# Output rows and probabilities turned by transposing transfers; the four score units of a tile in one block

## The chip, the cores and the metric

One core of a Trainium2 chip runs the whole program. The time is device microseconds from one launch to its end, a median over runs. Engines: TensorE (PE: products, and PEld, its weight loads), VectorE (DVE), ScalarE (ACT), GpSimd (POOL), and SyncE (SP), which here only issues transfers.

## The reference

One step of a one-layer decoder, for 2048 prompt tokens (16 tiles of 128) and 8 sample tokens:

```
u = rmsnorm(x) * g;  proj = u @ w_in          # 1024 -> 2832
GLA heads (4): per-token recurrence S = diag(a) S + k v^T, o = q S, in chunks; rmsnorm(o); * silu(gate)
window heads (8, two key heads): softmax over 128 keys back and a learned sink logit; * silu(gate)
h = x + concat(both) @ w_out;  y = rmsnorm(h) * g_final
```

It also returns the final states, keys and values. Tile n's window heads need the keys of tiles n-1 and n; the GLA state passes from tile to tile.

## The kernel before, in words

Each f32 operand of a large product is kept as two half-precision parts, hi and lo, and a product is three matmuls (`split_product`, L575 to L577: hi hi, hi lo, lo hi). All weights stay on chip. `iterations` runs `body(Tile(n))` for n = 0 to 14 on every engine, each engine in its own written order; semaphores tie them together (`Events`, `Ring`). Tile 0 has its own order (`early`), and the last tile is interleaved with the sample tokens after the loop.

In body t, PE projects the tile t+1 (`proj` of gqk, sq, sklow, gv, gg, sg) and does the attention of tile t between the projections, then the output projection of tile t (`out_proj`, two groups). The PSUM banks stand in three rings of two: `pj` for projections, `at_ring` for scores and outputs, `tr` for turned blocks. A block of a ring may be filled only when the block two places before it in the ring's list was read (`wait_free`), and the reader is named in the list: DVE for bc, sq and sklow, ACT for gqk, gv, gg and sg. `bc` (L580) spreads the inverse norms of tile t+2 over the partitions; `scale_u` and `split_u` make that tile's hi and lo input.

The window heads of a tile are four units of two heads. `scores` (L664) fills two units. DVE's `row_max` (L1587) moves the older keys in, scales and takes the maximum; ACT's `probs` (L1167) takes exponentials; PE turns the unit by a product with the identity (`turn_probs`, L686); ACT rounds the turned block to the hi part (`probs_hi`, L1176) and DVE takes the lo part and masks a copy (`take_pt`, L1608); `values` (L695) multiplies. There are two slots for units (u % 2), so units 0 and 1 pass before 2 and 3. The gated output rows are scaled by DVE (`scale_rows`, L1656), turned by PE (`turn_out`, L807), and split by ACT and DVE (`take_out`) into `ogT_hi` and `ogT_lo` for `out_proj`. SP loads x twice a tile (as rows for the norm, and transposed on the host), x again for the residual, and stores y.

## Time and profile before

| | before |
|---|---|
| median of 3 runs | 903.19 us (903.15 to 903.64) |
| the profiled execution | 904.62 us, span 902.8 us, mean granted clock 0.975 |
| PE busy | 881.7 us (98%) |
| PEld busy | 616.0 us (68%) |
| DVE busy | 687.9 us (76%) |
| ACT busy | 383.0 us (42%) |
| POOL busy | 77.5 us (9%) |
| chain that ended last | PE 88%, DVE 5%, issue 4%, DMA 2% |
| bytes moved | 56.55 MB, mean 63 GB/s |

Busy is the time in which an engine had an instruction of its own in flight; matmuls overlap, so a group's mean is longer than the step from one to the next. The chain that ended last is followed back from the last instruction through whatever released each step. Lines are those of the kernel printed above.

### The profile page before, as it was taken

The numbers are of one execution on the slowest core, as the hardware profiler recorded it, in microseconds if no ns is written. First come the engines' busy times: TensorE is split into PE (matmuls) and PEld (weight loads), VectorE is DVE, ScalarE is ACT, GpSimd is POOL, SyncE is SP. The second block draws the span as 40 slices with busy tenths as digits, with TensorE's granted clock in tenths as the row PEclk, the third lists the DMA queues.
The fourth block names the chain that finished last, engine by engine and source line by source line (L and its number), as shares of the span: only waits on it lengthen the run. The fifth ranks groups of instructions, "written<-read, shape, count | busy, mean of one in ns | idle before, by whom it ended". The sixth has DMA issues, their size and how long they took to land.

```text
span 902.8 us, 22427 instructions
## 1 busy us (share of the span) xinstructions
PE 881.7 (98%) x9066; PEld 616.0 (68%) x9066; DVE 687.9 (76%) x2223; ACT 383.0 (42%) x1008; POOL 77.5 (9%) x117
## 2 busy tenths in 40 slices
PE   7898999999999999999999999999999999999997
PEld 5884576675858576675858576675858676775775
DVE  5899678868787778868787777868777777876854
ACT  4564543435353443435353433534353533434411
POOL 0041010101010010101010000101010100101200
PEclk7999999999999999999999999999999999999976
DMA  9921002020110202020100202020200102020014
GB/s 376 379 95 71 1 2 94 2 94 1 47 50 1 94 1 95 2 95 1 64 32 6 89 2 95 2 94 1 92 5 25 71 2 94 2 74 25 3 71 155
DMA packets 15687, 56.55 MB, mean 63 GB/s; under 512 B 3746, under 2 KB 5210, under 8 KB 14561
## 3 DMA queue, kind: packets, MB, share of 16 engines
q1 hardware_dynamic: 15296, 55.05, 16.1%
q8 instruction: 72, 1.18, 0.5%
q14 instruction: 31, 0.25, 0.1%
q10 hardware_dynamic: 288, 0.07, 0.0%
HBM read 44.33 MB, written 10.78 MB: 61 GB/s over the span
## 4 chain that ended last, share of the span: by engine, by line
PE 88%; DVE 5%; issue 4%; DMA 2%; ACT 1%; POOL 0%; SPq 0%; POOLq 0%; DVEq 0%
PE bank L575 24%; PE bank L577 23%; PE bank L576 23%; PE bank L766 3%; PE bank L680 3%; PE bank L692 2%; PE bank L815 1%; PE bank L788 1%; PE bank L792 1%; PE bank L629 1%; PE bank L752 1%; DVE w_in_hi_lo L1758 1%; PE bank L803 1%; DMA w_out_hi<-in_w 1%; DMA x_rows<-in_xq 1%
## 5 line engine op out<-in xcount | busy, mean ns | idle before, releaser
L575 PE MATMUL bank<-u_hi,w_in_hi_lo 128*128 128x128 f16 (+1 forms) x1288 | 208.5, 214 | 3.6 <-DVE w_in_hi_lo L1758 2.8
L577 PE MATMUL bank<-u_hi,w_in_hi_lo 128*128 128x128 f16 (+1 forms) x1288 | 208.1, 214 | 0.0
L576 PE MATMUL bank<-u_lo,w_in_hi_lo 128*128 128x128 f16 (+1 forms) x1288 | 208.1, 214 | 0.0
L575 PE MATMUL bank<-w_in_hi_lo,u_hi 128*128 128x512 f16 (+3 forms) x528 | 176.5, 343 | 3.6 <-issue 3.6
L577 PE MATMUL bank<-w_in_hi_lo,u_lo 128*128 128x512 f16 (+3 forms) x528 | 176.5, 342 | 0.0
L576 PE MATMUL bank<-w_in_hi_lo,u_hi 128*128 128x512 f16 (+3 forms) x528 | 176.5, 342 | 0.0
L575 PEld LDWEIGHTS bank<-u_hi,w_in_hi_lo 128*128 128x128 f16 x1288 | 123.8, 98 | 16.3 <-issue 13.0
L576 PEld LDWEIGHTS bank<-u_lo,w_in_hi_lo 128*128 128x128 f16 x1288 | 123.6, 98 | 0.3
L577 PEld LDWEIGHTS bank<-u_hi,w_in_hi_lo 128*128 128x128 f16 x1288 | 123.6, 98 | 0.0
L575 PE MATMUL bank<-w_out_hi,ogT_hi 128*128 128x512 f16 x256 | 98.0, 383 | 0.5 <-DVE ogT_lo L1679 0.5
L576 PE MATMUL bank<-w_out_lo,ogT_hi 128*128 128x512 f16 x256 | 98.0, 383 | 0.0
L577 PE MATMUL bank<-w_out_hi,ogT_lo 128*128 128x512 f16 x256 | 97.8, 382 | 0.0
L577 PEld LDWEIGHTS bank<-w_in_hi_lo,u_lo 128*128 128x128 f16 (+1 forms) x528 | 52.0, 98 | 47.0 <-issue 1.1
L575 PEld LDWEIGHTS bank<-w_in_hi_lo,u_hi 128*128 128x128 f16 (+1 forms) x528 | 51.9, 98 | 45.5 <-issue 7.7
L1172 ACT ACTIVATE flex<-flex,win_stat 128x128 f32<-128x128 f32 x128 | 50.3, 393 | 73.2 <-DVE win_stat L1604 73.2
L576 PEld LDWEIGHTS bank<-w_in_hi_lo,u_hi 128*128 128x128 f16 (+1 forms) x528 | 52.0, 99 | 37.0 <-issue 0.8
L2089 POOL TENSOR_TENSOR flex<-flex,win_stat 128x512 f32<-128x512 f32 x16 | 16.7, 1044 | 441.5 <-DVE win_stat L1627 413.6
L1210 ACT CAST ogT_hi<-bank 128x512 f16<-128x512 f32 x32 | 17.2, 589 | 74.0 <-PE bank L815 74.0
L1476 DVE SCALAR_TENSOR_TENSOR win_q_hi_lo<-bank,win_q_hi_lo 128x512 f16<-128x512 f32 x16 | 11.0, 690 | 49.2 <-ACT win_q_hi_lo L1120 49.2
L1604 DVE CUSTOM_DVE_ANT_0 flex<-bank,band_bf,neg_sinks 128x128 f32<-128x128 f32 x128 | 47.0, 405 | 0.0
L577 PEld LDWEIGHTS bank<-w_out_hi,ogT_lo 128*128 128x128 f16 x256 | 25.3, 99 | 30.8 <-issue 1.1
L575 PEld LDWEIGHTS bank<-w_out_hi,ogT_hi 128*128 128x128 f16 x256 | 25.8, 101 | 29.8 <-issue 4.2
(303 smaller groups left out, 1740.2 us busy)
## 6 DMA issues: line engine op xcount, KB each, us to landing
xT<-in_xT SPq DMA_DIRECT2D x16, 512.0 KB, 4.9
x_rows<-in_xq SPq DMA_DIRECT2D x16, 512.0 KB
flex<-in_w SPq DMA_DIRECT2D x4, 2048.0 KB, 10.3
flex<-in_xq SPq DMA_DIRECT2D x16, 512.0 KB, 4.0
out_y<-flex SPq DMA_DIRECT2D x16, 512.0 KB, 2.6
w_out_lo<-in_w SPq DMA_DIRECT2D x2, 2048.0 KB, 12.4
w_out_hi<-in_w SPq DMA_DIRECT2D x1, 2048.0 KB, 10.0
w_out_hi<-in_w SPq DMA_DIRECT2D x1, 1088.0 KB, 7.5
```

The costliest lines, as they stand in the source:

```text
L575: nc.tensor.matmul(out, a_hi, b_hi, start=start and i == 0, stop=False)
L576: nc.tensor.matmul(out, a_hi, b_lo, start=False, stop=False)
L577: mm = nc.tensor.matmul(out, a_lo, b_hi, start=False, stop=stop and i == last)
L629: mm = nc.tensor.matmul(out[0:w, 0:w], top[:, d, c:c + w], top[:, d, c:c + w], start=d == 0 and c == 0, stop=d == DT - 1 and (c, w) == blo ...
L680: mm = nc.tensor.matmul(at_ring.bank(name, t)[:, i * 2 * P:(i + 1) * 2 * P], q16[r:r + HD, t.p, lq, 2 * pair + i, :], k16[r:r + HD, t.p, l ...
L692: tp = nc.tensor.transpose(bank[:, i * P:i * P + P], PR[:, u % 2, i, :], ident[:, :])
L766: mm = nc.tensor.matmul(bank[:, c:c + P], EX[:, l0 + l, f, :], QE[:, l0 + l, f].rearrange("p h c -> p (h c)"), start=True, stop=True)
L1172: e = nc.scalar.activation(PR[:, u % 2, i, :], PR[:, u % 2, i, :], ACT.Exp, scale=-1.0, bias=wst[:, 0, k:k + 1], accum_out=wst[:, 1, k:k + 1])
L1210: nc.scalar.copy(ogT_hi[:, 4 * g:4 * g + 4, 0:n], bank[:, :, 0:n]).then_inc(act_o.sem, 1)
L1476: V.scalar_tensor_tensor(out=q16[:, t.p, 1], in0=pj.bank("sq", t)[:, :].rearrange("p (f c) -> p f c", f=GRP), scalar=V_UNIT, in1=q16[:, t. ...
L1604: m = V.tensor_tensor_reduce(PR[:, u % 2, i, :], bank[:, i, P:2 * P], band[:, first], nsig[:, :], nsink[:, k:k + 1], ALU.add, ALU.min, wst ...
L2089: G.tensor_tensor(g, g, bcast(wst[:, 5, :], 2, HD), ALU.mult).then_inc(pool_w.sem, 1)
```

## The change

For tiles 1 to 14 (`on_pe` is true for 0 and 15 alone):

- The probabilities are not turned by PE. ACT rounds the unit's rows to the hi part (`rows_hi`), DVE takes the lo part (`rows_lo`), and SP issues a transposing transfer of both, 128x512 in half precision, from `pr16` into `PT` (`turn_prob_rows`). DVE then masks a copy (`mask_older`).
- The output rows are split before they are turned: ACT writes hi rows (`split_out`), DVE lo rows (in `scale_rows`), into `og_rows`, which is the memory of `x_rows`; two transposing transfers of 128x1024 (`turn_rows`) fill `ogT_hi` and `ogT_lo`. `out_proj` waits for both.
- `both_scores`: all four units are scored in one block, after the first of four features of sq. Units 2 and 3 lie in the two banks of `tr`.
- PE's order of a tile is sq (with the scores), sklow, bc, gv, ... , sg, gqk of tile t+2, out_proj. gqk was first, for tile t+1; bc was inside out_proj. `values` 2 and 3 come after both level products and the turned keys. The `pj` list follows.
- On ACT and DVE the steps around these are moved: `split_u`, `scale_u`, `take_qk`, `square_rows` and `norm_x` (now for t+3), `final_mean` and `final_scale`. On SP the loads of tile t+3 stand behind the four probability turns and the row turns, and y of tile t-1 is stored after the row turns of tile t.
- The `Ring` class takes the written list of fillings in place of a per-tile order; the waits it gives are again "two places before".
- `junk` shares the memory of `ogT_hi`.

The core of the diff:

```diff
+def on_pe(n):
+
+    return n in (0, NT - 1)
...
+        og_rows = xq[:, :].bitcast(F16).rearrange("p (l c) -> p l c", l=2)
...
-        junk = sb("junk", [P, D], BF16)
+        junk = ogT_hi[:, :, :].rearrange("p d c -> p (d c)").bitcast(BF16)
+        pr16 = sb("win_p_rows_hi_lo", [P, 2, 2, 2, P], F16)
...
+        for n in range(1, NT - 1):
+            pj_filled += [(u, n + ahead, reader[u]) for u, ahead in (
+                ("sq", 1), ("sklow", 1), ("bc", 2), ("gv", 1), ("gg", 1), ("sg", 1), ("gqk", 2))]
...
+        tr_filled = []
+        for n in range(NT):
+            if on_pe(n):
+                tr_filled += [(f"pt{u}", n, "dve") for u in range(4)]
+            else:
+                tr_filled += [("s2", n, "dve"), ("s3", n, "dve")]
+            tr_filled += [("KST", n, "act")]
+            if n < NT - 1:
+                tr_filled += [("glT", n, "act"), ("z", n, "dve"), ("SU", n, "dve")]
+            if on_pe(n):
+                tr_filled += [("og0", n, "dve"), ("og1", n, "dve")]
...
+            def store_y(t):
+                dve_f.wait(sp, "y", t)
...
+            def turn_rows(t):
+
+                at_ring.wait_full(sp, "y1", t + -1)
+                for l, (dst, ready) in enumerate(((ogT_hi, (act_o, "hi1")), (ogT_lo, (dve_o, "gsc1")))):
+                    ready[0].wait(sp, ready[1], t)
+                    sp.dma_start(dst[:, :, :], og_rows[:, l], transpose=True).then_inc(og_turned, 16)
+
+            def turn_prob_rows(t, u):
+
+                if u >= 2:
+                    pe_pv.wait(sp, f"pv{u - 2}", t)
+                else:
+                    pe_pv.wait(sp, f"pv{u + 2}", t + -1)
+                sp.wait_ge(pr_split, prob_unit(t, u))
+                sp.dma_start(PT[:, u % 2, 0].rearrange("p l h c -> p (l h) c"),
+                             pr16[:, u % 2].rearrange("p l h c -> p (l h c)"), transpose=True).then_inc(pr_turned[u % 2], 16)
+
...
             def body(t):
...
+                else:
+                    for u in range(4):
+                        turn_prob_rows(t, u)
+                    if t.n + 3 <= NT:
+                        load_xT(t + 3)
+                    turn_rows(t)
+                    store_y(t + -1)
+                    sp.wait_ge(og_turned, 32 * t.n)
+                    if t.n + 3 <= NT:
+                        load_xq(t + 3)
+                    load_xres(t)
...
+            def both_scores(t):
+                scores(t, 0)
+                scores(t, 1)
...
                     at_ring.wait_free(pe, name, t)
                 if g == 0 and d0 == 0:
-                    tr.wait_freed(pe, "og1", t)
+                    if on_pe(t.n):
+                        tr.wait_freed(pe, "og1", t)
+                    else:
+                        pe.wait_ge(og_turned, 32 * t.n)
...
@@ -973,54 +1021,62 @@
...
                 else:
+                    proj(nxt, "sq", between={0: [(both_scores, t)]})
                     proj(nxt, "sklow")
+                    bc(t + 2)
                     proj(nxt, "gv", 4)
-                values(t, 0)
-                values(t, 1)
-                if early:
                     leaf_scores(t)
-                turn_probs(t, 2)
-                turn_probs(t, 3)
...
+                    values(t, 1)
                     proj_rest(nxt, "gv", 4)
-                values(t, 2)
-                level_scores(t, "L1", 0)
-                values(t, 3)
-                level_scores(t, "L2", 2)
-                turn_keys(t)
-                turn_low(t)
+                    level_scores(t, "L1", 0)
+                    level_scores(t, "L2", 2)
+                    turn_keys(t)
+                    turn_low(t)
+                    values(t, 2)
+                    values(t, 3)
                 proj(nxt, "gg", 3)
...
+                else:
+                    proj(nxt, "sg")
+                    proj(t + 2, "gqk")
+                    out_proj(t, 0)
+                    out_proj(t, 1)
...
             def take_gate(t, g):
                 n, name = t.tokens, ("gg", "sg")[g]
                 pj.wait_full(act, name, t)
-                if g == 0 and not (t.static and t.off == 0):
-                    tr.wait_full(act, "og1", t + -1)
+                if g == 0 and t.n > 0:
+                    if on_pe(t.n - 1):
+                        tr.wait_full(act, "og1", t + -1)
+                    else:
+                        dve_o.wait(act, "gsc0", t + -1)
+                if g == 1 and t.n > 0 and not on_pe(t.n - 1):
+                    dve_o.wait(act, "gsc1", t + -1)
                 nc.scalar.activation(gates[0:n, g * 512:g * 512 + 512], pj.bank(name, t)[0:n, :], ACT.Silu,
...
+            def rows_hi(t, u):
+
+                if prob_unit(t, u) > 2:
+                    act.wait_ge(pr_turned[u % 2], turned_count(t, u) - 16)
+                act_w.wait(act, f"p{u}", t)
+                nc.scalar.activation(pr16[:, u % 2, 0], PR[:, u % 2], ACT.Identity, scale=P_TOP
+                                     ).then_inc(act_p.sem, 1)
...
+            def split_out(t):
+
+                dve_o.wait(act, "rscs", t)
+                for g in range(2):
+                    c = slice(g * 512, g * 512 + 512)
+                    nc.scalar.activation(og_rows[:, 0, c], gates[:, c], ACT.Identity, scale=amax[:, 1:2]
+                                         ).then_inc(act_o.sem, 1)
+
...
@@ -1318,27 +1395,29 @@
...
+                else:
+                    for u in range(4):
+                        probs(t, u)
+                        rows_hi(t, u)
+                    take_sq(nxt)
+                    final_root(t + -1)
                 sink_term(t)
+                if not early:
+                    split_u(t + 2)
...
+                else:
+                    split_out(t)
+                    nc.scalar.preload_act_table_set(SILU_SET)
...
+                else:
+                    take_qk(t + 2)
+                    if t.n + 3 <= NT:
+                        square_rows(t + 3)
+                        norm_rows(t + 3)
+                    final_square(t)
...
+            def rows_lo(t, u):
+
+                act_p.wait(dve, f"h{u}", t)
+                V.scalar_tensor_tensor(out=pr16[:, u % 2, 1], in0=PR[:, u % 2], scalar=P_TOP, in1=pr16[:, u % 2, 0],
+                                       op0=ALU.mult, op1=ALU.subtract).then_inc(pr_split, 1)
+
+            def mask_older(t, u):
+
+                dve.wait_ge(pr_turned[u % 2], turned_count(t, u))
+                V.tensor_tensor(PT[:, u % 2, 1].rearrange("p l h c -> p (l h) c"),
+                                PT[:, u % 2, 0].rearrange("p l h c -> p (l h) c"), bcast(older16[:, :], 1, 4),
+                                ALU.mult).then_inc(dve_p.sem, 1)
...
                 dve_o.wait(dve, "rsc", t)
+                V.tensor_scalar(a[:, 1:2], a[:, 3:4], O_TOP, None, ALU.mult).then_inc(dve_o.sem, 1)
+                dve_o.wait(dve, "rscs", t)
                 for g in range(2):
-                    c = g * 512
-                    V.tensor_scalar(gates[0:n, c:c + 512], gates[0:n, c:c + 512], a[:, 3:4], O_TOP, ALU.mult,
-                                    ALU.mult).then_inc(dve_o.sem, 1)
+                    c = slice(g * 512, g * 512 + 512)
+                    if on_pe(t.n):
+                        V.tensor_scalar(gates[:, c], gates[:, c], a[:, 1:2], None, ALU.mult).then_inc(dve_o.sem, 1)
+                    else:
+                        act_o.wait(dve, f"hi{g}", t)
+                        V.scalar_tensor_tensor(out=og_rows[:, 1, c], in0=gates[:, c], scalar=a[:, 1:2],
+                                               in1=og_rows[:, 0, c], op0=ALU.mult, op1=ALU.subtract
+                                               ).then_inc(dve_o.sem, 1)
                 V.tensor_scalar(isc[0:n, :], inv[0:n, NG - 2:NG], a[:, 2:3], 1.0 / O_TOP, ALU.mult, ALU.mult
...
@@ -1968,52 +2079,71 @@
...
                 else:
                     row_max(t, 0)
                     row_max(t, 1)
...
+                    rows_lo(t, 0)
+                    row_max(t, 2)
+                    rows_lo(t, 1)
+                    row_max(t, 3)
+                    final_mean(t + -1)
+                    take_sq(nxt)
+                    rows_lo(t, 2)
+                    rows_lo(t, 3)
                     sink_steps(t)
...
+                    mask_older(t, 0)
+                    mask_older(t, 1)
                     take_kv(nxt)
-                take_pt(t, 3)
-                assemble_leaves(t)
-                if not early:
-                    sink_steps(t)
-                denominators(t)
+                    scale_u(t + 2)
+                    mask_older(t, 2)
+                    mask_older(t, 3)
+                    assemble_leaves(t)
+                    denominators(t)
                 assemble_levels(t)
...
+                else:
+                    split_u(t + 2)
                 gate_window(t)
...
+                else:
+                    final_scale(t + -1)
...
+                else:
+                    split_v(nxt)
+                    if t.n != NT - 2:
+                        factors(nxt)
+                    if t.n + 3 <= NT:
+                        mean_square(t + 3)
+                        norm_x(t + 3)
+                    residual(t)
```

## Rows read from the trace of the kernel before

**Rows 1.** Engine busy time and granted clock, core 0: one tile, then fourteen tiles.
```profile
380.60:431.00 50.40, 50.36 (x503) 34.62 (x501) 39.27 (x130) 21.41 (x60) 3.56 (x6) 1.00 0.11 43
128.60:834.00 705.40, 704.15 (x7030) 482.98 (x7030) 544.18 (x1803) 299.53 (x843) 50.78 (x88) 1.00 0.12 43
```

**Rows 2.** PE in order of time, one tile: start us, us, what.
```profile
381.17 0.83 PE L680 MATMUL bank<-win_k_hi_lo,win_q_hi_lo 64*128 64x256 f16 x12
381.93 0.23 PE L575 MATMUL bank<-u_hi,w_in_hi_lo 128*128 128x128 f16 x1
...
388.60 0.23 PE L575 MATMUL bank<-u_hi,w_in_hi_lo 128*128 128x128 f16 x1
...
389.95 0.23 PE L575 MATMUL bank<-w_in_hi_lo,u_hi 128*128 128x144 f16 x1
...
391.45 0.38 PE L575 MATMUL bank<-w_in_hi_lo,u_hi 128*128 128x512 f16 x1
...
394.04 0.19 PE L575 MATMUL bank<-win_v_hi_lo,flex 128*128 128x64 f16 x1
...
394.74 0.63 PE L692 MATMUL bank<-ident,flex 128*128 128x128 f32 x4
395.30 0.72 PE L752 MATMUL bank<-flex 64*128 64x128 f32 x8
395.95 0.39 PE L575 MATMUL bank<-w_in_hi_lo,u_hi 128*128 128x512 f16 x1
...
412.51 1.04 PE L815 MATMUL bank<-ident,flex 128*128 128x128 f32 x8
413.38 0.38 PE L575 MATMUL bank<-w_in_hi_lo,u_hi 128*128 128x512 f16 x1
```

**Rows 3.** ACT and DVE in order of time, the same tile.
```profile
387.50 0.60 ACT L1120 ACTIVATE win_q_hi_lo<-bank 128x512 f16<-128x512 f32 x1 [1.97 <-PE bank L577]
...
388.13 0.69 DVE L1476 SCALAR_TENSOR_TENSOR win_q_hi_lo<-bank,win_q_hi_lo 128x512 f16<-128x512 f32 x1 [3.51 <-ACT win_q_hi_lo L1120]
...
391.57 0.15 DVE L1597 COPY win_stat<-neg_sinks 128x1 f32<-128x1 f32 x1
...
392.82 0.16 DVE L1404 TENSOR_TENSOR h_stat<-h_stat 128x1 f32<-128x1 f32 x1
...
392.94 0.40 ACT L1172 ACTIVATE flex<-flex,win_stat 128x128 f32<-128x128 f32 x1 [0.37 <-DVE win_stat L1604]
...
393.63 0.18 ACT L1172 ACTIVATION_READ_ACCUMULATOR flex<-flex,win_stat 128x1 f32 x1
...
396.07 0.42 DVE L1615 TENSOR_TENSOR flex<-flex,older_slot 128x512 f16<-128x512 f16 x1
396.41 0.28 DVE L1446 TENSOR_SCALAR win_k_hi_lo<-bank 128x128 f16<-128x128 f32 x1
...
397.25 0.41 DVE L1611 SCALAR_TENSOR_TENSOR flex<-bank,flex 128x256 f16<-128x256 f32 x1
...
411.17 0.88 DVE L1670 TENSOR_SCALAR flex<-flex,row_max 128x512 f32<-128x512 f32 x2
...
414.57 1.28 ACT L1127 ACT_TABLE_LOAD   x1
...
424.74 1.23 DVE L1439 TENSOR_TENSOR u_lo<-xT,u_hi 128x1024 f16<-128x1024 f32 x1 [1.11 <-ACT u_hi L1097]
```

**Rows 4.** DMA issues: KB of one, median us from issue to landing.
```profile
xT<-in_xT SPq DMA_DIRECT2D x16, 512.0 KB, 4.9
out_y<-flex SPq DMA_DIRECT2D x16, 512.0 KB, 2.6
...
out_Sp<-gla_state SPq DMA_DIRECT2D x4, 32.0 KB, 2.1
```

**Rows 5.** Busy time and granted clock around two idle stretches of PE.
```profile
24.00:28.00 4.00, 1.21 (x17) 0.95 (x15) 3.96 (x12) 0.04 (x1) 0.00 (x0) 1.00 0.98 319
28.00:32.00 4.00, 4.00 (x45) 4.00 (x45) 3.96 (x14) 3.62 (x2) 0.00 (x0) 0.57 1.13 428
```

More of the change, by code:

```diff
@@ L65 @@
 LOG_EXP_SET = "natural_log_exp_and_others"
+SILU_SET = "silu_and_others"
 PREP = [2, 0, 1, 3, 4, 5, 6, 7]
@@ L115 @@
 class Ring:
-    def __init__(self, banks, full, freed, order, tail=None, head=None, last=None):
-        self.banks, self.full, self.freed, self.order = banks, full, freed, order
-        self.last = order if last is None else last
-        self.tail = order if tail is None else tail
-        self.head = [(u, n) for n in range(2) for u, _ in order] if head is None else head
-    def _list(self, t):
-        if t.static and t.off == NT - 1:
-            return self.last
-        return self.tail if t.sample else self.order
@@ L133, in _index, with __init__ @@
-    def _index(self, name, t):
-        return [u for u, _ in self._list(t)].index(name)
-    def _in_head(self, t):
-        return t.static and t.off < 2
+    def __init__(self, banks, full, freed, filled):
+        self.banks, self.full, self.freed = banks, full, freed
+        self.filled = [(name, n) for name, n, _ in filled]
+        count = {who: 0 for who in freed}
+        self.place, self.release = {}, {}
+        for i, (name, n, who) in enumerate(filled):
+            count[who] += 1
+            self.place[name, n] = i
+            self.release[name, n] = who, count[who]
@@ L170, in wait_free @@
+        eng.wait_ge(self.freed[who], rank)
+    def wait_free(self, eng, name, t):
+        i = self.place[name, t.n]
         if i >= 2:
-            self.wait_freed(eng, self._list(t)[i - 2][0], t)
-        else:
-            self.wait_freed(eng, self.order[len(self.order) + i - 2][0], t + -1)
+            before, n = self.filled[i - 2]
+            self.wait_freed(eng, before, Tile(n))
+def on_pe(n):
+    return n in (0, NT - 1)
 def bcast(ap, axis, n):
@@ new lines, in hymba_step_kernel @@
+        pj_filled = [(u, n, reader[u]) for u, n in (
+            ("bc", 0), ("sklow", 0), ("bc", 1), ("gqk", 0), ("sq", 0), ("sklow", 1), ("gv", 0), ("gqk", 1), ("sq", 1),
+            ("gv", 1), ("gg", 0), ("sg", 0), ("gg", 1), ("sg", 1), ("bc", 2), ("gqk", 2))]
+        for n in range(1, NT - 1):
+            pj_filled += [(u, n + ahead, reader[u]) for u, ahead in (
+                ("sq", 1), ("sklow", 1), ("bc", 2), ("gv", 1), ("gg", 1), ("sg", 1), ("gqk", 2))]
+        pj_filled += [(u, NT, who) for u, who in (
+            ("kt", "act"), ("sklow", "act"), ("low", "act"), ("z", "dve"),
+            ("gates", "act"), ("sq", "act"), ("kv0", "dve"), ("kv1", "dve"), ("sc", "act"),
+            ("kv2", "dve"), ("pT", "dve"), ("kv3", "dve"), ("o", "dve"), ("pv", "dve"), ("ss", "dve"),
+            ("y", "dve"), ("hs", "dve"))]
@@ new lines, in hymba_step_kernel @@
+        pj = Ring(banks[0:2], sem("proj_full"), {"act": sem("proj_freed_act"), "dve": sem("proj_freed_dve")}, pj_filled)
+        at_ring = Ring(banks[2:4], sem("attn_full"), {"dve": sem("attn_freed_dve")},
+                       [(u, n, "dve") for n in range(NT) for u in (
+                           "s0", "s1", "s2", "s3", "leaf0", "leaf1", "L1", "L2", "y0", "y1")
+                        if on_pe(n) or u not in ("s2", "s3")])
+        tr_filled = []
[9 more added lines that the diff above has]
+                tr_filled += [("og0", n, "dve"), ("og1", n, "dve")]
@@ L1349, in body @@
                 take_low(t)
-                if not (t.static and t.off + 2 > NT):
+                if early:
                     square_rows(t + 2)
@@ L1970, in body @@
                     sums(t)
+                    take_sq(nxt)
+                    take_pt(t, 0)
+                    take_pt(t, 1)
+                    row_max(t, 2)
+                    row_max(t, 3)
+                    sink_steps(t)
+                    dve.wait_ge(init, 2)
+                    factors(t)
+                    take_pt(t, 2)
+                    take_pt(t, 3)
+                    assemble_leaves(t)
+                    denominators(t)
                 else:
```

227 lines of the change are left out of this document (98 added, 129 removed).

## The prediction

> **What bounds the kernel now.** I read the busy time by stretch first, then TensorE (PE) in order of time over one tile, then ScalarE (ACT) and VectorE (DVE) over the same tile, then the DMA issues. The middle of the program is fourteen equal tiles of 50.40 us, and PE is busy 50.36 us of each at a granted clock of 1.00, while DVE has 39.27 and ACT 21.41 [rows 1]. So a matmul that goes gives its whole length, and any wait of PE that comes in costs its whole length: there is no slack on PE to hide it. The reader is to see in rows 2 that one group's start follows the end of the last, and in rows 3 that DVE and ACT finish each step in time only because PE has other work between a product and its next use.
>
> **What it removes.** In the fourteen tiles 1 to 14 PE no longer turns probabilities and output rows. Four turned blocks fill 394.74 to 395.30, 0.56 us, and there are eight in a tile, so 1.1 us; the eight output blocks fill 412.51 to 413.38, 0.87 us [rows 2]. Together 1.97 us a tile, 27.6 us in fourteen. Tiles 0 and 15 keep theirs. The other products keep their numbers and lengths, so a tile of PE without waits is 50.40 - 1.97 = 48.43 us.
>
> **What it adds on PE: the new order against the two projection banks.** A bank may be filled when the block two places before it in the list has been read. The list is now sq, sklow, bc, gv, gg, sg, gqk. So bc waits for DVE's take_sq, and gv, right behind, for take_kv. Before, gv waited for take_sq (done 388.82 [rows 3], wanted 391.45 [rows 2]: 2.6 us of slack) and take_kv was wanted only by gg. I lay the new tile out from 0, where PE starts sq.
> PE: one feature of sq is 24 matmuls, 388.60 to 389.95, 1.35 us; a pair of score units 381.17 to 381.93, 0.76; sklow 388.60 to 391.45, 2.85; half of gv 391.45 to 394.04, 2.59; leaves 395.30 to 395.95, 0.65 [rows 2]. So the first pair of scores ends at 2.11, sq at 1.35 + 1.52 + 4.05 = 6.92, sklow at 9.77, and there PE asks for bc.
> DVE: row_max starts at 2.2 and one takes 1.25 (391.57 to 392.82; ACT starts on it at 392.94, 1.37 after DVE did [rows 3]). ACT's exponentials of a unit take 392.94 to 393.81, 0.87 [rows 3]; its new cast rows_hi of 256 numbers I take at 0.4, under the 0.60 of the 512 wide one [rows 3]. A rows_lo or a mask_older is taken at the 0.34 from 396.07 to 396.41 [rows 3]. Then: row_max 0 to 3.45, row_max 1 to 4.7, rows_lo 0 (after the cast at 4.9) to 5.3, row_max 2 to 6.55, rows_lo 1 to 6.9, row_max 3 to 8.15. ACT: exponentials of unit 2 to 7.55; its cast must wait until transfer 0 has read the same slot. Transfer 0 goes out at 5.35 and lands X later.
> X is not in the trace: no transfer turns anything. Bounds: 2.1 us (32 KB out of SBUF) and 4.9 (512 KB with a rearranged row, into SBUF); between them 2.6 (512 KB out of SBUF) [rows 4]. A unit is 128 KB. I take 2.6, the row nearest in that it reads SBUF in long rows. Farther out than 4.9 lies the case that each block of 128 columns costs such a time by itself, below.
> With 2.6: cast 2 at 7.95 to 8.35, exponentials 3 to 9.25, cast 3 (slot free at 6.95 + 2.6 = 9.55) to 9.95, ACT's q copy 0.60 to 10.6, DVE's take_sq 0.69 to 11.3 [rows 3]. PE's bc starts 11.35 instead of 9.77: **first wait, 1.6 us**. On DVE then stand rows_lo 2 and 3, sink_steps, mask_older 0 and 1 (1.5 us), and take_kv, 396.41 to 397.25, 0.84 [rows 3]: it ends 13.6. PE is through with bc at 11.55 and can start gv at 13.7: **second wait, 2.1 us**. This one hardly depends on X, for transfer 1 has landed by 9.55.
> gv and leaves end at 16.95, values 0 at 17.3. The SyncE (SP) queue sends turn 2 only after values 0, so it lands near 20.1 and turn 3 near 20.6. mask_older 2 and 3 stand on DVE ahead of assemble_leaves, which alone frees the bank of L1: it is free at 21.3. PE has values 1 and the rest of gv until 20.25: **third wait, 1.1 us** at X = 2.6, none below 1.5.
> **Fourth wait.** DVE's split_u (1.23 [rows 3]) now lies ahead of scale_rows, ACT splits the rows (two of 0.6) and loads a table (1.28), and only then reads gg, which frees the bank of gqk. DVE's scaling now starts at 411.17 [rows 3] + 0.8; + 0.1 + 1.1 + 1.28 + 0.6 of the read gives 415.1 on the old time line; PE with no turns stands there at 412.51 [rows 2] + 9 x 0.216 = 414.45. Taken at 0.75, between 0 and 1.2.
> The output transfers start where the scaling ends and have sg's tail and the whole of gqk (5.4 us, four features) ahead of out_proj, so PE covers them up to some 6 us; without that cover each microsecond counts. SP's own queue (four turns, xT, two row turns, store, two loads) is free for the rest of the tile: one issue takes a fraction of a microsecond and all waits in it but pv0 and pv1 are old by then. The residual and the norm of tile t+3 lie beside out_proj; I count them as nothing, and about 1 us each tile if DVE comes late to the residual.
> Sum of waits 1.6 + 2.1 + 1.1 + 0.75 = 5.55 us; tile 48.43 + 5.55 = 54.0 us, +3.6.
>
> **The clock.** Between 24 and 28 us PE was idle 2.8 of 4 us with two tiny products between the gaps, and then ran at 0.57 of full clock over 28 to 32 (mostly the 1.2 GHz level) [rows 5]: 0.43 x 4 = 1.7 us lost. The first two waits leave PE idle 3.7 of 4 us with only bc (0.2) between. Bounds 0 (the clock holds) and 1.7; I take 1.7, for the gap here is larger than the one in the trace. Tile 55.7, +5.3.
> Head and tail: same work in another order, 0 within 2 us. The profiled execution took 904.62 around a span of 902.8, 0.16% over the median 903.19. 14 x 5.33 = 74.6, on 904.62 it is 979.2, as a median 978.
>
> **What the skill says of X.** Its page "VectorE: DVE Perf Modes", section "The three transpose paths", gives 1309 ns for one turned 128x128 block of 2 bytes by DMA; four in a row would be 5.2 us for a unit, an estimate from that page, and the sum would then be well over 1040. "Advanced Engine Details and Errata", section "X-Bar Transpose (TRN2)", says a turning DMA is as fast as an ordinary one, which would leave X at the rows above and the sum as it is. No run so far shows either.
>
> **Rivals.**
> (a) *The turn is slow.* X = 4.9 as the xT row: cast 2 at 10.25, cast 3 at 11.85, take_sq done at 13.5: first wait 3.7; second 2.1; third 1.1 + 2.3 = 3.4; fourth 0.75; 9.95 in all, + 1.7 of the clock - 1.97 = 9.7 a tile, 136 us: 1039. If the transfers of a unit also queue behind each other by half of X, 1060. For it: a unit is turned in 2-byte pieces. Against: 128 KB is little.
> (b) *The turn is quick or the clock holds.* X = 2.1: waits 1.3, 2.1, 0.6, 0.7 = 4.7, clock full: +2.7 a tile, 941. With the third and fourth wait gone too it is 3.4 - 1.97 = 1.4, 923. For it: PE's gaps are each under 2.2 us. Against: rows 5.
> (c) *Faster.* PE's 1.97 us come through: the banks are read in time. It needs the chain row_max, exponentials, casts, q copy, take_sq, masks, take_kv to end 3.9 us sooner than laid out (take_kv by 9.9 instead of 13.6), or at least all waits of a tile under 1.97 us, which is the point from which it decides. With none left: 903.2 - 27.6 = 876. For it: DVE stood idle 3.51 us before take_sq in the old tile [rows 3]. Against: that idle time is now filled by two row_max and two rows_lo, whose lengths are measured.
>
> **Chances.** The forecast with its neighbourhood (957 to 1005) 0.42, (a) 0.22, (b) 0.22, (c) 0.11, and 0.03 for waits that equal the gain. About 0.2% is what a measurement of this kernel can tell from none. Faster 0.11, within 0.2% 0.02, slower 0.87. Range 925 to 1060: from (b) with its short form to (a) with queueing; it leaves out (c) and turns of over 5 us. The forecast's own range is 957 to 1005.
>
> **What would show it.** In the profile after: a middle tile of 54 to 56 us instead of 50.40; PE idle before bc's product (L585) with DVE's take_sq as the one waited for, before gv with take_kv, before L1 with the leaf assembly; SP issues of turned units about 1.7 us apart for 0 and 1, and the other two only behind values 0; granted clock under 1.00 in the middle slices. Wrong if PE is busy all through the tile, if a tile takes under 50 us, or if the output turn is what PE waits for ahead of out_proj.

## The result and the profile after

The changed kernel takes 997.48 us (993.85 to 999.2) against 903.17 us of the kernel before on the same chip: 1.1043 times as long, 95% interval 1.1008 to 1.1078. Over the fourteen tiles that turn by transfer it is 94.3 / 14 = 6.7 us more each, a mean tile of 50.40 [rows 1] + 6.7 = 57.1 us.

| | after |
|---|---|
| the profiled execution | 999.2 us, span 997.4 us, mean granted clock 0.945 |
| PE busy | 884.9 us (89%) |
| DVE busy | 675.3 us (68%) |
| ACT busy | 390.6 us (39%) |
| bytes moved | 71.22 MB, mean 71 GB/s |

The page of the profile after, from its second and fourth part: the granted clock by slice, the packets, and the shares of the chain that ended last.

```profile
PEclk7999989989899999999898998989899999989997
DMA packets 75717, 71.22 MB, mean 71 GB/s; under 512 B 63777, under 2 KB 65241, under 8 KB 74592
...
PE 51%; DVE 25%; DMA 9%; issue 6%; ACT 6%; SPq 2%; POOL 0%; POOLq 0%; ACTq 0%; DVEq 0%
```

The chain was 88% PE before; now 42% of it runs over DVE, transfers, ACT and SP's issues. Which waits do that is in the waits of PE, after (who was waited for: us in total, times, longest):

```profile
PE bank L625 <- DVE win_q_hi_lo L1566: 31.5, 14, 3.2
PE bank L811 <- DVE flex L1629: 25.0, 14, 2.8
PE bank L615 <- DVE g_low_hi_lo_hi L1548: 23.8, 14, 1.9
PE bank L615 <- ACT flex L1188: 8.2, 13, 0.6
```

Each row is one of the four waits of the forecast: L625 is bc behind take_sq (2.25 us a tile), L615 behind L1548 is gv behind take_kv (1.7), L811 is L1 behind assemble_leaves (1.8), and the last is gqk behind ACT's read of gg (0.6 in the thirteen tiles that have it). Together 88.5 / 14 = 6.3 us a tile. One tile in order of time, after, where [rows 2, 3] show the same steps of before:

```profile
421.24 0.42 ACT L1252 ACTIVATE win_p_rows_hi_lo<-flex 128x256 f16<-128x256 f32 x1 [1.03 <-DMA flex<-win_p_rows_hi_lo]
...
422.67 0.42 ACT L1252 ACTIVATE win_p_rows_hi_lo<-flex 128x256 f16<-128x256 f32 x1 [0.25 <-DMA flex<-win_p_rows_hi_lo]
423.00 0.58 ACT L1176 ACTIVATE win_q_hi_lo<-bank 128x512 f16<-128x512 f32 x1
...
423.61 0.69 DVE L1566 SCALAR_TENSOR_TENSOR win_q_hi_lo<-bank,win_q_hi_lo 128x512 f16<-128x512 f32 x1 [2.67 <-ACT win_q_hi_lo L1176]
...
424.35 0.49 PE L625 MATMUL bank<-rstd_diag,ones 128*128 128x128 f32 x2 [1.94 <-DVE win_q_hi_lo L1566]
...
426.39 0.17 DVE L1548 SCALAR_TENSOR_TENSOR g_low_hi_lo_hi<-bank,g_low_hi_lo_hi 128x16 f16<-128x16 f32 x1
...
426.61 0.39 PE L615 MATMUL bank<-w_in_hi_lo,u_hi 128*128 128x512 f16 x1 [1.77 <-DVE g_low_hi_lo_hi L1548]
...
434.61 0.42 DVE L1719 TENSOR_TENSOR flex<-flex,older_slot 128x512 f16<-128x512 f16 x1 [6.00 <-DMA flex<-win_p_rows_hi_lo]
435.93 0.42 DVE L1719 TENSOR_TENSOR flex<-flex,older_slot 128x512 f16<-128x512 f16 x1 [0.89 <-DMA flex<-win_p_rows_hi_lo]
436.27 0.75 DVE L1629 TENSOR_TENSOR flex<-bank,leaf_mask 128x256 f32<-128x256 f32 x2
...
436.75 0.82 PE L811 MATMUL bank<-flex 128*128 128x128 f32 x5 [1.64 <-DVE flex L1629]
```

The brackets are to be read backwards. PE's bc stood idle 1.94 us for take_sq (L1566); DVE had been idle 2.67 us for ACT's q copy (L1176); ACT had come to it behind two casts that both waited for a turn (1.03 and 0.25 us; the rest of the 2.67 is ACT's own work on units 2 and 3). Lower down, two masks wait for turns 2 and 3 and hold assemble_leaves (L1629), which has waited for nothing of its own, and so PE's L1.

The third loss is the clock, in the busy time by stretch, after (length, then busy us and number of PE, PEld, DVE, ACT, POOL, then granted clock, DMA share, GB/s):

```profile
414.80:471.40 56.60, 50.62 (x487) 33.12 (x485) 38.31 (x128) 22.03 (x60) 3.56 (x6) 0.97 0.24 57
427.00:428.00 1.00, 1.00 (x6) 0.36 (x4) 1.00 (x5) 0.00 (x0) 0.00 (x0) 0.70 0.00 0
428.00:429.00 1.00, 1.00 (x4) 0.44 (x3) 0.62 (x3) 0.35 (x1) 0.00 (x0) 0.50 0.00 0
429.00:430.00 1.00, 1.00 (x4) 0.30 (x2) 0.00 (x0) 0.70 (x1) 0.00 (x0) 0.50 0.00 0
430.00:431.00 1.00, 1.00 (x5) 0.16 (x3) 0.00 (x0) 0.00 (x0) 0.00 (x0) 0.59 0.00 0
135.00:835.00 700.00, 620.14 (x5875) 404.54 (x5872) 466.92 (x1569) 268.20 (x736) 42.76 (x72) 0.95 0.22 56
```

After the two idle stretches before bc and gv PE runs at 0.50, the 1.2 GHz level: 0.30 + 0.50 + 0.50 + 0.41 = 1.7 us lost in this tile. Over all of the middle the clock is 0.95. What a mean tile has beyond work and waits is 57.1 - 48.4 - 6.3 = 2.4 us. The tiles are not alike in this; two of them, from one bc to the next:

```profile
368.70:424.40 55.70, 48.96 (x484) 32.79 (x484) 38.39 (x129) 21.92 (x60) 3.57 (x6) 1.00 0.23 58
481.70:539.80 58.10, 51.36 (x483) 33.26 (x483) 38.33 (x129) 21.99 (x60) 3.57 (x6) 0.94 0.22 56
```

Of thirteen such stretches between 141.3 and 885.2 us eight have a clock of 0.94 (about 3.4 us lost), four 0.97 (1.7) and one 1.00.

The first wait differs by tile too, from 1.4 to 3.2 us, and it follows the landing of turns 0 and 1. At 307 us both land after 2.4 us and PE then waits 1.41; at 591 us one of them takes 4.2 and PE waits 3.17:

```profile
312.86 0.49 PE L625 MATMUL bank<-rstd_diag,ones 128*128 128x128 f32 x2 [1.41 <-DVE win_q_hi_lo L1566]
...
L544 SPq DMA_TRANSPOSE flex<-win_p_rows_hi_lo x2: 1188/1190/1192, 590.8 to 592.4; - x2
DMA to landing us min/median/max: 2.4/3.3/4.2
...
598.30 0.79 PE L625 MATMUL bank<-rstd_diag,ones 128*128 128x128 f32 x2 [3.17 <-DVE win_q_hi_lo L1566]
```

In five of the fourteen tiles both land within 2.7 us, and the wait is 1.4 to 1.7; in the other nine one of the two takes 3.1 to 4.2, and the wait is 1.9 to 3.2. Why they are late there is not shown.

### The profile page after: what moved, and what is told of

Same layout as the page of the kernel before. It is cut to its first block, busy times and chain, and to the rows that moved or that the text cites. A ratio compares the mean times of both kernels' runs of the same rounds, so it can differ in the third digit from the quotient of the medians.

```text
span 997.4 us, 22021 instructions
## 1 busy us (share of the span) xinstructions
PE 884.9 (89%) x8842; PEld 592.9 (59%) x8842; DVE 675.3 (68%) x2211; ACT 390.6 (39%) x1008; POOL 77.6 (8%) x117
## 2 busy tenths in 40 slices
DMA packets 75717, 71.22 MB, mean 71 GB/s; under 512 B 63777, under 2 KB 65241, under 8 KB 74592
## 4 chain that ended last, share of the span: by engine, by line
PE 51%; DVE 25%; DMA 9%; issue 6%; ACT 6%; SPq 2%; POOL 0%; POOLq 0%; ACTq 0%; DVEq 0%
PE bank L615 15%; PE bank L616 14%; PE bank L617 14%; DMA flex<-win_p_rows_hi_lo 8%; PE bank L811 3%; SPq L544 2%; DVE x_rows L1780 2%; DVE gla_state L1673 2%; DVE win_p_rows_hi_lo L1713 2%; DVE u_lo L1529 2%; DVE flex L1756 2%; DVE flex L1719 2%; ACT flex L1233 1%; DVE flex L1695 1%; PE bank L721 1%
## 5 line engine op out<-in xcount | busy, mean ns | idle before, releaser
L615 PE MATMUL bank<-u_hi,w_in_hi_lo 128*128 128x128 f16 (+1 forms) x1288 | 208.5, 214 | 11.1 <-ACT flex L1188 8.2
L615 PE MATMUL bank<-w_in_hi_lo,u_hi 128*128 128x512 f16 (+3 forms) x528 | 186.7, 362 | 27.4 <-DVE g_low_hi_lo_hi L1548 23.8
L616 PE MATMUL bank<-w_in_hi_lo,u_hi 128*128 128x512 f16 (+3 forms) x528 | 186.4, 362 | 0.0
L617 PE MATMUL bank<-w_in_hi_lo,u_lo 128*128 128x512 f16 (+3 forms) x528 | 185.3, 360 | 0.0
L615 PEld LDWEIGHTS bank<-u_hi,w_in_hi_lo 128*128 128x128 f16 x1288 | 123.8, 98 | 23.1 <-ACT flex L1188 15.2
L615 PEld LDWEIGHTS bank<-w_in_hi_lo,u_hi 128*128 128x128 f16 (+1 forms) x528 | 53.6, 102 | 78.1 <-DVE g_low_hi_lo_hi L1548 26.9
L615 PE MATMUL bank<-w_out_hi,ogT_hi 128*128 128x512 f16 x256 | 98.2, 383 | 0.7 <-DVE ogT_lo L1790 0.6
L1719 DVE TENSOR_TENSOR flex<-flex,older_slot 128x512 f16<-128x512 f16 x56 | 22.5, 422 | 102.8 <-DMA flex<-win_p_rows_hi_lo 102.8
L617 PEld LDWEIGHTS bank<-w_in_hi_lo,u_lo 128*128 128x128 f16 (+1 forms) x528 | 54.0, 102 | 53.8 <-issue 13.0
L616 PEld LDWEIGHTS bank<-w_in_hi_lo,u_hi 128*128 128x128 f16 (+1 forms) x528 | 53.7, 102 | 44.0 <-issue 10.5
L811 PE MATMUL bank<-flex 128*128 128x128 f32 x256 | 33.0, 282 | 25.0 <-DVE flex L1629 25.0
L1800 DVE SCALAR_TENSOR_TENSOR flex<-bank,row_unscale,flex 128x512 f32<-128x512 f32 x32 | 23.8, 748 | 39.3 <-PE bank L617 35.3
L811 PEld LDWEIGHTS bank<-flex 128*128 128x128 f32 x256 | 29.9, 191 | 32.3 <-DVE flex L1629 31.9
L1292 ACT ACTIVATE ogT_hi<-flex 128x1024 bf16<-128x1024 f32 x16 | 16.9, 1058 | 79.4 <-DVE flex L1800 79.4
```

The lines of the kernel that those rows point to most:

```text
L615: nc.tensor.matmul(out, a_hi, b_hi, start=start and i == 0, stop=False)
L616: nc.tensor.matmul(out, a_hi, b_lo, start=False, stop=False)
L617: mm = nc.tensor.matmul(out, a_lo, b_hi, start=False, stop=stop and i == last)
L811: mm = nc.tensor.matmul(bank[:, c:c + P], EX[:, l0 + l, f, :], QE[:, l0 + l, f].rearrange("p h c -> p (h c)"), start=True, stop=True)
L1719: V.tensor_tensor(PT[:, u % 2, 1].rearrange("p l h c -> p (l h) c"), PT[:, u % 2, 0].rearrange("p l h c -> p (l h) c"), bcast(older16[:, : ...
L1800: V.scalar_tensor_tensor(out=x, in0=at_ring.bank(f"y{g}", t)[0:n, :], scalar=isc[0:n, g:g + 1], in1=x, op0=ALU.mult, op1=ALU.add).then_inc ...
```

## The experiments

The theory after the result: the 6.7 us a tile (6.3 of waits and 2.4 beyond them, less the 2.0 of products that are gone) are for the most part three places in the written order (take_sq behind casts that wait for turns, take_kv behind masks, assemble_leaves behind masks), and the clock that the first two cost. The rivals: the turning transfers themselves are slow, whatever the order; or the clock is most of it. Each experiment was timed beside the kernel before, whose medians were 902.5 to 902.8 us. "The waits" are those of PE, for the four sources above.

**Each place alone, then all three.** `e1_sq_early` takes the q block between the units:

```diff
-                    for u in range(4):
+                    for u in range(2):
                         probs(t, u)
                         rows_hi(t, u)
                     take_sq(nxt)
+                    for u in range(2, 4):
+                        probs(t, u)
+                        rows_hi(t, u)
```

and on DVE take_sq ahead of `row_max(t, 3)`. 

> Edit: take_sq of the next tile is done on ACT after units 0 and 1 and on DVE ahead of row_max 3, where it stood behind all four units. Theory (bank order): bc no longer waits (its bank is read at about 8.4 us of the tile, PE asks at 9.8), but take_kv still stands behind row_max 3 and the masks, so PE's wait in front of gv grows from 1.8 us to about 3 us and only 0.5 to 1.1 us a tile are won: 980 to 991 us. The clock loss stays, for the one gap is now as long. Rival (the waits are independent prices that add up): 2.25 us a tile come back, 966 us. Rival (the transfers' time is what is paid): no change, 997 us.

Measured: 986.20 us (982.69 to 989.64), ratio 1.092 (1.0881 to 1.0958). The waits of PE in it:

```profile
PE bank L615 <- DVE g_low_hi_lo_hi L1551: 43.8, 14, 3.5
PE bank L811 <- DVE flex L1632: 24.6, 14, 2.9
PE bank L615 <- ACT flex L1188: 8.2, 13, 0.6
```

bc no longer waits (31.5 before the edit), but gv waits 43.8 instead of 23.8. Two thirds of the first wait moved into the second; what went is 88.5 - 76.6 = 11.9 us of waits, and the time fell by 11.3. The clock over 135 to 835 us is 0.96: with one idle stretch of 3.1 us a tile in this place it falls nearly as far as with two in a row.

`e2_kv_first` moves `take_kv(nxt)` on DVE to right behind `take_sq(nxt)`:

```diff
                     take_sq(nxt)
+                    take_kv(nxt)
                     rows_lo(t, 2)
...
                     mask_older(t, 1)
-                    take_kv(nxt)
```

> Edit: DVE does take_kv right behind take_sq, ahead of rows_lo 2 and 3 and of masks 0 and 1. Theory (bank order): PE's wait in front of gv falls from 1.8 to about 0.4 us; the one in front of bc stays at 2.2. That is 1.4 us a tile, 977 us; if the clock now holds in part of the tiles, because PE's idle stretch is shorter, down to 945 us. Rival (the transfers' time is what is paid): masks 0 and 1 and with them values 0 come no earlier, so PE waits in front of values or L1 instead and the time stays within 5 us of 997.

Measured: 967.96 us (959.92 to 969.93), ratio 1.0701 (1.0653 to 1.0749).

```profile
PE bank L625 <- DVE win_q_hi_lo L1566: 30.9, 14, 3.1
PE bank L811 <- DVE flex L1629: 24.7, 14, 2.5
PE bank L615 <- ACT flex L1188: 8.2, 13, 0.6
PE bank L615 <- DVE g_low_hi_lo_hi L1548: 4.3, 12, 0.5
```

The waits fell by 20.4 us and the time by 29.5. The clock over 135 to 835 us rose to 0.98: with the second of the two idle stretches nearly gone, part of the clock came back.

`e3_leaves_first` has the leaves and denominators ahead of the last two masks:

```diff
+                    assemble_leaves(t)
+                    denominators(t)
                     mask_older(t, 2)
                     mask_older(t, 3)
-                    assemble_leaves(t)
-                    denominators(t)
```

> Edit: DVE takes the leaf blocks and the denominators ahead of masks 2 and 3, so that the bank of L1 doesn't wait for turns 2 and 3. Theory (bank order): PE's wait in front of L1, 1.8 us a tile, goes; masks 2 and 3 are ready at 19 to 21 us of the tile and values 2 and 3 are wanted at about 24, so nothing comes in its place: 1.8 to 2.4 us a tile, 963 to 972 us, the clock loss in front of gv as it was. Rival (the turns are late for everybody): values 2 then wait for turn 3 and at most 0.5 us a tile are won, 990 us or more.

Measured: 970.49 us (970.09 to 970.99), ratio 1.0746 (1.0729 to 1.0763); the wait of L811 is gone, the other three stand at 30.6, 24.6 and 8.1. The leaves have nothing to do with the probabilities; only their place in DVE's queue tied PE to turns 2 and 3.

`e4_all_three` is these edits together (take_kv then stands behind take_sq and `row_max(t, 3)`). 

> Edit: the three moves together (take_sq early, take_kv behind it, leaves ahead of masks 2 and 3). The transposing transfers are all there. Theory (bank order): of the four waits only 0.5 to 1 us in front of gv and 0.6 us in front of gqk are left, and the clock holds with gaps so short: a tile of 49.3 to 50.0 us, 886 to 897 us, faster than the kernel before at 903. Rival (the transfers' time is what is paid): the tile stays over 53 us, above 940 us. Rival (the clock falls however short the gaps): some 910 to 925 us with a granted clock of 0.95 in the middle tiles.

Measured: 896.17 us (892.28 to 898.35), ratio 0.9918 (0.9891 to 0.9944).

```profile
PE bank L615 <- DVE g_low_hi_lo_hi L1551: 10.8, 14, 1.0
PE bank L615 <- ACT flex L1188: 8.1, 13, 0.6
```

101 us came back, and the three edits alone give 11 + 30 + 27 = 68. Of the 33 us more, 12 are waits: 69.6 us of them went here, against 11.9 + 20.4 + 25.2 = 57.5 in the three alone, because the part that `e1_sq_early` only moved in front of gv goes too. The other 21, and 10 of the 68, came back beyond the waits: together 32 us, 2.3 a tile, which is the size of the remainder of 2.4. The clock is 1.00 over 135 to 835 us here, where the three edits alone had 0.96 to 0.98. The order of the readers is the cause of the loss; with it mended, all transfers in place, the change is 0.8% faster than the kernel before.

**The transfer itself.** `e5_plain` issues all six transfers of a tile without `transpose=True`, the same bytes between the same places; the turning is left out.

```diff
-                    sp.dma_start(dst[:, :, :], og_rows[:, l], transpose=True).then_inc(og_turned, 16)
+                    sp.dma_start(dst[:, :, :].rearrange("p d c -> p (d c)"), og_rows[:, l]).then_inc(og_turned, 16)
```

and likewise for the four of the probabilities. 

> Edit: all six transfers of a tile that turn their data are plain copies of the same bytes between the same buffers, so probabilities and output rows reach the products unturned (this part of the computation is left out); all waits and the order stay as in the changed kernel. Theory (bank order first, turn time second): an issue falls from 1.2 us to some 0.4 and a landing from 2.4 to about 2 us, so casts 2 and 3 and turns 2 and 3 come earlier and the waits in front of bc and L1 shrink by 0.7 to 1.5 us each, while the one in front of gv stays: 955 to 976 us. Rival (the turning is what is paid): the tile falls to that of the matmuls, under 900 us. Rival (the turn's length doesn't matter at all): within 5 us of 997.

Measured: 970.25 us (967.28 to 973.13), ratio 1.0747 (1.071 to 1.0784). In this order, turning costs 27 of the 94 us; the rest of the loss stands without it. What it costs once the order is mended was not run. The line that issues the probability transfers, in the changed kernel (ns of SP min/median/max, first and last start, and below it from issue to landing):

```profile
L544 SPq DMA_TRANSPOSE flex<-win_p_rows_hi_lo x56: 1188/1201/2387, 134.3 to 894.8; - x56
...
DMA to landing us min/median/max: 2.4/2.4/4.2
```

and in `e5_plain`:

```profile
L544 SPq DMA_DIRECT2D flex<-win_p_rows_hi_lo x56: 464/471/1373, 135.0 to 867.2; - x56
...
DMA to landing us min/median/max: 1.9/2.0/3.7
```

The turning transfer lands 0.4 us later and holds SP 0.7 us longer, so the second of a pair comes 1.1 us later than a plain one. These are medians: late landings of units 0 and 1 (about 3 us and more) are in nine tiles with turning and in four without. The waits in `e5_plain` say the same: bc 20.9 instead of 31.5, L1 8.6 instead of 25.0, gv 25.0, which never hung on a turn.

**The clock by itself.** `e6_fill` leaves the order and puts 30 products of 128x128 before bc and 26 before gv, into a bank that nobody reads then (`fill`, not shown); their results are not used.

```diff
                     proj(nxt, "sklow")
+                    fill(t, 30)
                     bc(t + 2)
+                    fill(t, 26)
                     proj(nxt, "gv", 4)
```

> Edit: PE does 30 matmuls of 128x128 (about 1.7 us) before it waits for bc's bank and 26 (1.45 us) before it waits for gv's, into a bank that is free then; the results are not used. They fit into the first two waits, 2.25 and 1.7 us a tile. Theory (the gaps cost the clock as well): the granted clock of the middle tiles, 0.95 as the changed kernel has it, goes to about 1.00 and 1.7 to 2.8 us a tile come back although PE does more: 955 to 975 us, and the waits for DVE that are left add up to under 1 us a tile. Rival (the clock falls for another reason, the transfers or the wait before L1): no gain, 995 to 1005 us at 0.95.

Measured: 975.17 us (973.14 to 976.15), ratio 1.0799 (1.0775 to 1.0822), at the upper edge of what was expected. Its busy time over the middle:

```profile
135.00:835.00 700.00, 657.56 (x6829) 454.24 (x6827) 485.36 (x1621) 278.43 (x761) 45.28 (x76) 1.00 0.23 58
```

The clock is 1.00 against 0.95, although a wait of 1.7 us in front of L1 is still there in every tile. The waits fell from 88.5 to 44.4 us, and the 56 products take 56 x 1.35 / 24 = 3.2 us a tile (24 of them take 1.35, [rows 2]), 44 us: the filling took the place of the waiting, and the 22.3 us that came back, 1.6 a tile, are the clock's. The traces say it more closely. PE over thirteen tiles from bc to bc, in the changed kernel, in `e6_fill`, and in `e7_leaf_between` (below), whose only waits of the four are those for gg:

```profile
141.30:885.20 743.90, 662.10 (x6279) 432.30 (x6279) 498.01 (x1665) 285.56 (x780) 46.32 (x78) 0.95 0.21 55
...
141.10:857.80 716.70, 675.50 (x7007) 466.19 (x7007) 498.29 (x1665) 285.52 (x780) 46.32 (x78) 1.00 0.22 57
...
138.10:776.20 638.10, 628.50 (x6284) 427.49 (x6281) 499.84 (x1665) 285.63 (x780) 46.24 (x78) 1.00 0.25 64
```

PE is busy 662.1 / 13 = 50.9 us a tile in the changed kernel and 675.5 / 13 - 3.15 = 48.8 in `e6_fill` without the filling: the same products take 2.1 us longer at the lower clock. (The medians give less, 1.6; the profiled execution of the changed kernel is 1.7 us above its median and that of `e6_fill` 2.0 below.) The last 0.5 of busy time, 48.8 against 48.3 in `e7_leaf_between`, is there at full clock, where PE stops up to four times a tile instead of once; how it comes about is not shown.

**What is left, and two steps further.** `e7_leaf_between` is `e4_all_three` with `leaf_scores(t)` between bc and gv on PE. 

> Edit: on top of the three moves (896 us), PE does leaf_scores between bc and gv, where it waits 0.8 us a tile for take_kv; the leaf scores are 0.65 us of work in other banks. Theory (bank order): that wait falls to about 0.15 us: 0.6 us a tile, 887 to 889 us. Rival (values 0 or another step is the real limit of this stretch): the wait comes back in front of values 0, within 2 us of 896.

Measured: 888.29 us (887.28 to 889.12), ratio 0.984 (0.9818 to 0.9862). The wait before gv is gone, and of the four only that for ACT's read of gg is left, 8.2 us in 13 tiles.

`e8_split_late` takes that one on: DVE's `split_u(t + 2)` stands behind the scaling of the rows.

```diff
-                else:
-                    split_u(t + 2)
                 gate_window(t)
...
                 else:
+                    split_u(t + 2)
                     final_scale(t + -1)
```

> Edit: e7_leaf_between and, with it, DVE's split_u of tile t+2 behind scale_rows, so that the scaling, ACT's row split and the read of gg come 1.2 us sooner. Theory (fourth wait): PE's 0.6 to 1.1 us in front of gqk go, and u_lo of tile t+2 is just ready in time: another 8 to 14 us, 874 to 881 us. Rival (u_lo is then what PE waits for in front of gqk): nothing is won over e7, 887 us, the wait now for split_u.

Measured: 902.05 us (900.39 to 908.64, ten runs), ratio 0.9995 (0.9975 to 1.0015): 14 us slower where 7 to 14 faster was expected. The expectation was wrong. The waits of PE in it:

```profile
PE bank L615 <- DMA ogT_lo<-x_rows: 14.9, 11, 2.6
PE bank L615 <- DVE u_lo L1532: 5.1, 13, 0.4
```

The wait for ACT is gone, as meant. In its place PE waits for the output turn, for which it had waited at most once in a run so far (1.7 us in `e7_leaf_between`). DVE and SP in order of time, the same kernel:

```profile
461.50 1.41 DVE L1783 SCALAR_TENSOR_TENSOR x_rows<-flex,row_max,x_rows 128x512 f16<-128x512 f32 x2 [0.86 <-ACT x_rows L1286]
...
462.96 1.22 DVE L1532 TENSOR_TENSOR u_lo<-xT,u_hi 128x1024 f16<-128x1024 f32 x1
...
464.20 0.33 SPq L484 DMA_DIRECT2D xT<-in_xT  x1
464.63 1.24 SPq L535 DMA_TRANSPOSE ogT_hi<-x_rows  x1
```

The first scaled rows (hi, by ACT) are there at 462.0 and the others at 462.9, but the turn goes out at 464.63. In SP's queue the load of xT for tile t+3 stands ahead of it, and that load overwrites what split_u reads, which now ends at 464.2. `e9_turn_first` swaps the two in SP's queue and changes nothing else:

```diff
-                    if t.n + 3 <= NT:
-                        load_xT(t + 3)
                     turn_rows(t)
+                    if t.n + 3 <= NT:
+                        load_xT(t + 3)
```

> The kernel of e8_split_late, with SP issuing the two output turns ahead of the load of tile t+3. Theory: in e8 the load stood in SP's queue ahead of the output turns and waited for the late split of u, so the turns, whose rows were ready 1.7 us earlier, landed late and PE waited 1.3 us a tile for them. Then the 14.9 us of PE waiting for ogT_lo go, 902 - 15 = 887, or less by up to 4: 883 to 887. Rival: the turn is late because DVE scales the rows late, and the queue has no part: 898 to 903.

Measured: 884.03 us (883.21 to 884.84), ratio 0.9797 (0.9781 to 0.9812). The wait for the output turn is gone from the fourteen tiles but for one of 1.9 us, and 5.0 us for u_lo is all that is left of the order. This is the fastest version of the case, 2.0% (1.9 to 2.2) under the kernel before and 11% under the changed one.

**How far the waits hang on the turn.** Two kernels issue each probability turn twice, the second after the first has landed, the changed one and `e7_leaf_between` (the waits for a turn, in `rows_hi` and `mask_older`, count both; not shown):

```diff
                 sp.dma_start(PT[:, u % 2, 0].rearrange("p l h c -> p (l h) c"),
                              pr16[:, u % 2].rearrange("p l h c -> p (l h c)"), transpose=True).then_inc(pr_turned[u % 2], 16)
+                sp.wait_ge(pr_turned[u % 2], turned_count(t, u) * 2 - 16)
+                sp.dma_start(PT[:, u % 2, 0].rearrange("p l h c -> p (l h) c"),
+                             pr16[:, u % 2].rearrange("p l h c -> p (l h c)"), transpose=True).then_inc(pr_turned[u % 2], 16)
```

> The changed kernel, with each of the four probability turns of a tile issued twice, the second after the first has landed, into the same place. Theory (the first and third wait hang on the turn, one for one): turns 0 and 2 land about 3 us later, turns 1 and 3 about 6 us later; the first wait grows by 4 to 6, the third by 5 to 7, the second stays; 9 to 13 a tile more with their clock, 126 to 182: 1123 to 1180. Rival (the waits come from the order of DVE's and ACT's work and the turn is beside it): under 1040.

Measured: 1162.89 us (1158.84 to 1168.38), ratio 1.2884 (1.283 to 1.2938). PE's waits in it:

```profile
PE bank L628 <- DVE win_q_hi_lo L1569: 92.2, 14, 7.8
PE bank L814 <- DVE flex L1632: 91.8, 14, 7.2
PE bank L618 <- DVE g_low_hi_lo_hi L1551: 20.9, 14, 1.9
PE bank L618 <- ACT flex L1191: 8.1, 13, 0.6
```

The first and third wait grow by 4.3 and 4.8 us a tile and the second does not, so these two hang on the turn's time (the third was expected to grow by 5 to 7). The time rose by 11.8 a tile, the last 2.9 of it with the clock, whose mean over the middle is 0.88.

> The kernel of e7_leaf_between with the same doubling of the four probability turns. Theory: bc, gv and L1 no longer hang on a turn, so the doubling reaches PE only through the masks 2 and 3 and what stands on DVE behind them, and costs under a third of what it costs in e10: 0 to 4 us a tile, 888 to 945. Rival (the slack was thin, and the doubled turn comes back in full, 9 a tile or more): 1010 and over.

Measured: 1011.92 us (1010.64 to 1013.81), ratio 1.1216 (1.1195 to 1.1236). Here the rival was right in size: the doubling costs 124 us, 8.8 a tile, against 165 in `e10_twice_old`. The first three waits stay away, but a new one stands there:

```profile
PE bank L618 <- DVE flex L1725: 79.6, 29, 3.9
```

It is `values` waiting for the masked units (L1725 is the mask), twice a tile: 2.9 us in front of values 0 and 3.9 in front of values 3 in the tile at 434 us. That is 5.7 of the 8.8; the clock over the middle is 0.94 where `e7_leaf_between` has 1.00, and the rest goes with it. The expectation had only masks 2 and 3 in the path; masks 0 and 1 are in it as well. The better order freed bc, gv and L1 from the turn, but not the product that uses it, and that one had less slack than I took it to have.

## Why the prediction held

Forecast 978 us, measured 997.5: inside the range and inside the forecast's own range (957 to 1005), by the mechanism named. Two terms came out too small, the first wait and the clock. With the tile laid out from row_max 0 (2.2 in the forecast, 414.82 in the trace, so 0 is 412.62), the steps compare directly:

| step | forecast | measured |
|---|---|---|
| PE asks for bc | 422.4 | 422.4 (424.35 - 1.94) |
| cast of unit 2 | 420.6 | 421.24 |
| cast of unit 3 | 422.2 | 422.67 |
| take_sq done | 423.9 | 424.3 |
| take_kv done | 426.2 | 426.6 |
| first wait | 1.6 | 2.25 |
| second | 2.1 | 1.7 |
| third | 1.1 | 1.8 |
| fourth | 0.75 | 0.6 |
| clock | 1.7 | 2.4 beyond the waits, 2.1 of it the clock |
| tile | 55.7 | 57.1 |

- *The removal* of 1.97 us a tile and the layout from rows of the old tile held to some tenths; PE is busy 628.5 / 13 = 48.3 us a tile in `e7_leaf_between`, where the forecast has 48.43 without waits. From its time one gets 50.40 - 14.3 / 14 = 49.4 a tile, 0.3 more than the 49.1 that the trace shows for the middle tiles; that part lies outside of them or in the spread of the executions.
- *X.* Taken at 2.6, one value for all. The median landing is 2.4, but one of turns 0 and 1 takes 3.1 to 4.2 in nine of fourteen tiles, and that is what the first wait has above the forecast: 1.4 to 1.7 in the five other tiles, where 1.6 was forecast. In the tile of the table turn 0 lands after 3.1, and ACT's cast of unit 2 starts 3.2 us after DVE's low part of unit 0 ended (418.04). The other term that was mis-sized is SP's issue, "a fraction of a microsecond" in the forecast; it is 1.2 us for a turned unit, and the pair of turns 2 and 3 comes 1.3 us apart (masks at 434.61 and 435.93) where the forecast had 0.5. That is about the 0.7 us by which the third wait is longer.
- *The second wait* hardly depends on X: so it was (20.9 in `e10_twice_old`, 25.0 in `e5_plain`, 23.8 in the changed kernel). It came out smaller for the first came out larger; together they are 3.95 against 3.7.
- *The clock.* The argument from [rows 5] held in direction: two gaps with 0.5 us of product between them (0.2 in the forecast), then the lower level. Its size is in part luck. The forecast bounded the loss at 1.7; eight of thirteen tiles lose 3.4, four 1.7, and one nothing, with gaps of 1.40 and 1.77 us (at 368.7 and 371.0), much like the tile of the table. What decides between these is not shown.
- *The output turn* is hidden, as said: PE waits for it in no middle tile of the changed kernel. `e8_split_late` shows how thin the cover is, and where: in SP's queue, not in the transfer.
- *Rivals.* (a), the slow turn, is out: 2.4 us, and without the turning 970.25 us, still 67 us over the kernel before. (b), the clock holds, is out for this kernel, and `e6_fill` shows what it would have been worth. (c), faster, needs what `e4_all_three` does: the takers of the banks not queued behind the turns. Then PE's 1.97 us come through in part (6.6 of 27.6 us in `e4_all_three`), and for the most part after three more moves (18.5 in `e9_turn_first`). Order alone had nothing to win in the kernel before, whose PE was busy 50.36 of 50.40 us [rows 1].
- The issue-to-landing time of 2.4 us can be held against both rules weighed for X. The Trainium skill, "VectorE: DVE Perf Modes", section "The three transpose paths", has 1309 ns for a 128x128 block; four of them would be 5.2, an estimate from that page, and the trace doesn't agree for a transfer that holds four. The Trainium skill, "Advanced Engine Details and Errata", section "X-Bar Transpose (TRN2)", has a turning DMA as fast as an ordinary one; the traces come near that for the landing of a unit (2.4 against 2.0), less so for the 128x1024 rows (3.2 against 2.3), and not for the issue (1.20 against 0.47).

## What to carry to other kernels

When work moves from a full engine to a transfer, the gain is the engine's time, but the price is set by who stands behind the new wait in the queues of the other engines: list them, and move what doesn't need the transfer ahead of it before judging the transfer. The same step must be done on the queue that issues transfers, where a load that waits for a reader holds back all behind it. Idle stretches of PE can cost the clock on top of their length: here 1.9 and 1.8 us with 0.5 us of product between them did, and so did one of 3.1 us (`e1_sq_early`), so removing them gave more than the waits themselves (101 us for 69.6 of waits in `e4_all_three`). And look at the spread of a transfer's landings, not at the median alone: the late ones set the first wait here.
